# Prompt attention: normalising the softmax weights before their transposes instead of the outputs after the value products

## The chip, the cores and the metric

One core of one Trainium2 chip. The metric is device time in microseconds of one execution of the whole kernel, which computes one inference step of a one-layer hybrid encoder. All data are float32.

## The reference, cut to what matters

The layer has two parallel groups of heads, an output projection and a feed-forward block. The change touches only the prompt part of the attention group: 8 heads, 1,024 queries, 1,040 keys (16 learned tokens and 1,024 frames), block-causal by chunks of 64.

```python
def attend_block(qn, qr, q_chunk, kn, kr, v, k_chunk):
    s = jnp.einsum('bqhd,bkhd->bhqk', qn, kn) + jnp.einsum('bqhr,bkr->bhqk', qr, kr)
    s = s.astype(jnp.float32) * ATTN_SCALE
    mask = k_chunk[None, :] <= q_chunk[:, None]
    s = jnp.where(mask[None, None], s, NEG)
    p = jax.nn.softmax(s, axis=-1).astype(v.dtype)
    return jnp.einsum('bhqk,bkhd->bqhd', p, v)
```

The outputs of all heads then pass through an RMS norm and, beside the other group's outputs, the output projection.

## The kernel before, in words

The kernel has three stages, one after the other: `layer_inputs` (input projection, the recurrent heads, the sample's attention), `prompt_attention` and `tail` (output projection and feed-forward block). The change is in `prompt_attention`.

**Tiles and steps.** Heads are taken in four pairs. A step is one head of the pair (`a`, 0 or 1) and one tile of 128 queries (`t`, 0 to 7). Tile `t` sees `144 + 128 t` keys (`width[t]`), cut into 1 score unit for tiles 0 to 2, 2 units for tiles 3 to 6 and 3 units for tile 7. A pair has 16 steps in an order written out by hand, which puts a long tile beside a short one:

```python
ORDER = ((0, 7), (0, 0), (1, 7), (0, 1), (0, 6), (1, 0), (1, 6), (1, 1),
         (0, 5), (0, 2), (1, 5), (0, 3), (0, 4), (1, 2), (1, 4), (1, 3))
MIX = ((3, 7), (0, 10), (2, 15), (1, 18))
LAG, BANKS, TURN = 2, 5, 5
```

**What a step does.** TensorE multiplies queries and keys (L1937) into one of five PSUM banks, queries on partitions; the mask comes with eight extra rows of the operands. VectorE takes each row's maximum (L2100 for one unit; L2102 for each of several and L2105 over them). ScalarE writes the exponentials to `pq` and their sum for each unit to `sums` (L2024). TensorE transposes the weights by 128x128 blocks, in groups of up to four (L1949), into banks 5 and 6, and VectorE and ScalarE copy the groups to `pT` (L2012 and L2017): for tiles 4 to 7 ScalarE the first and third group and VectorE the second, for tiles 0 to 3 VectorE the first and ScalarE any other.

**The value products.** For two query tiles at once (`m` = 0 to 3) and both heads of the pair, `mix` multiplies V and the transposed weights into bank 7 (L1967); the output has the two heads' 64 values on partitions and 256 queries in columns. There are four in a pair, 16 in all, placed by `MIX` after the steps 7, 10, 15 and 18, counted from the first step of the pair.

**Normalisation.** Queries are columns there, while the sums lie with queries on partitions. So VectorE adds the parts of the sums for two tiles and two heads (L2113) and takes reciprocals (L2115). GpSimd widens each reciprocal to 64 columns (`wide`, L2076). TensorE transposes `wide` into the other half of bank 7, two transposes before each value product (L1958). ScalarE copies that half to `spread` (L2017, called by `widened`). VectorE multiplies output and `spread` into `g.mixT` (L2119).

**The order of work around it.** Each engine runs its instructions in order and waits on semaphores. In iteration i of the loops, TensorE does scores(i), the transposes of step i-2, then a value product if one is placed there. VectorE does the maxima of step i, its copies for step i-2, sums and reciprocals of a pair of tiles just finished, and the output multiplication of a value product one iteration older. ScalarE does its copies for step i-2, the exponentials of step i, then the copy of `spread`. Steps share four slots of maxima (`RINGS`). SyncE's queue loads the next heads' V after `m_ps` has counted the last value product of a pair.

Behind these loops, ScalarE squares each pair's outputs (L2036), GpSimd adds the squares up (L2061), TensorE sums them over partitions and already does the other group's part of the output projection (L1974); VectorE multiplies the outputs by the norm (L2141).

Of the kernel before, what the change touches and what calls it, by code (L numbers as in the profile page):

```python
# [11 lines left out]
P = 128  # L12
# [1802 lines left out]
def prompt_attention(nc, g, io, phase):  # L1815
# [19 lines left out]
    part = sb("part", [P, RINGS, 3])  # L1835
    neg = sb("neg", [P, RINGS])
    sums = sb("sums", [P, 2, QT_N, 2, 3])
    total = sb("total", [P, 2, QT_N, 2])
    rec = sb("rec", [P, 2, QT_N, 2])
    wide = [sb(f"wide{i}", [P, 2 * P]) for i in range(2)]  # L1840
    spread = [sb(f"spread{i}", [P, 2 * P]) for i in range(2)]
    sq = sb("sq", [P, SEQ])
    acc = sb("acc", [P, SEQ])
    norm = sb("norm", [P, QT_N])
# [33 lines left out]
    ready = {}  # L1878
    for pair in range(PAIRS):
        for j, (m, _) in enumerate(MIX):  # L1880
            last = max(x for x, (_, t) in enumerate(ORDER) if t // 2 == m)
            ready.setdefault(pair * len(ORDER) + last, []).append((pair, m, 4 * pair + j))
    done_at = {n: i for i, found in ready.items() for _, _, n in found}
    END = max(mixes) + 1
    s = {n: sem("a_" + n) for n in """qk_in0 qk_in1 qk_in2 qk_in3 v_in0 v_in1 v_in2 v_in3 rw_in m_in fixed s_ps part_ok neg_ok e_ok t_ps
        ta_ok tv_ok tot_ok rec_ok wide_ok m_ps sp_ok o_ok sq_ok acc_ok ss_ps ms_ok pow_ok bc_ps mix_ok zero new_ok wo_in""".split()}
    block = phase.block()

    def turned(n):
# [37 lines left out]
    def _(pe):  # L1927
# [12 lines left out]
        def turns(i):  # L1940

            _, a, t = steps[i]
            pe.wait_ge(s["e_ok"], unit_at[i + 1])
            for j, (k0, k1) in enumerate(groups[i]):
                n = group_at[i] + j
                if n >= 2:
                    pe.wait_ge(*turned(n - 2))
                for k in range(k0, k1):
                    last = pe.transpose(pb[TURN + n % 2][:, (k - k0) * P:(k - k0 + 1) * P], rows_of(a, t)[:, k * P:(k + 1) * P], ident)  # L1949
                last.then_inc(s["t_ps"], 1)  # L1950

        def mix(pair, m, n):
            out, done = pb[7], group_at[done_at[n] + 1]
            pe.wait_ge(s["wide_ok"], n + 1)
            if n:
                pe.wait_ge(s["o_ok"], n)
            for x in range(2):
                pe.transpose(out[:, 2 * P + x * P:3 * P + x * P], wide[n % 2][:, x * P:x * P + P], ident)  # L1958
            pe.wait_ge(s["ta_ok"], act_before[done])
            pe.wait_ge(s["tv_ok"], done - act_before[done])  # L1960
            for a in range(2):
                head = 2 * pair + a
                pe.wait_ge(s[f"v_in{head % 4}"], head // 4 * 32 + 32)
            for k in range(2 * m + 3):
                x = max(0, P * k - CHUNK - 2 * P * m)
                for a in range(2):
                    last = pe.matmul(out[64 * a:64 * a + 64, x:2 * P], vh[(2 * pair + a) % 4][0:size[k], k, :],  # L1967
                                     cols_of(a, m)[0:size[k], k, x:], start=k == 0, stop=True, skip_group_check=k > 0)
            last.then_inc(s["m_ps"], 1)
# [45 lines left out]
    @block.scalar  # L2015
    def _(act):
        copy = lambda out, in_: act.activation(out, in_, ACT.Copy)  # L2017

        def weights(i):
            pair, a, t = steps[i]  # L2020
            act.wait_ge(s["neg_ok"], i + 1)
            for u in range(units[i]):
                n, x, y = unit_at[i] + u, cuts[t][u], cuts[t][u + 1]
                act.activation(rows_of(a, t)[:, x:y], pb[n % BANKS][:, 0:y - x], ACT.Exp, bias=neg[:, i % RINGS:i % RINGS + 1],  # L2024
                               accum_out=sums[:, pair % 2, t, a, u:u + 1]).then_inc(s["e_ok"], 1)

        def widened(n):
            act.wait_ge(s["m_ps"], n + 1)
            copy(spread[n % 2][:, :], pb[7][:, 2 * P:4 * P]).then_inc(s["sp_ok"], 1)

        def squares(j):
            act.wait_ge(s["o_ok"], 4 * j + 4)
            if j:
                act.wait_ge(s["acc_ok"], j)
            out = sq if j else acc
            act.activation(out[:, :], g.mixT[:, j, 0:SEQ], ACT.Square).then_inc(s["sq_ok"], 1)  # L2036

        for b in range(4):
            rows = slice(QKD, ROWS)
            q0, k0 = CON["q_mask"][0], CON["k_mask_rows"][0]  # L2040
            act.dma_start(qT[b][rows, :], io.con[rows, q0:q0 + SEQ]).then_inc(s["m_in"], 16)
            act.dma_start(kT[b][rows, :], io.con[rows, k0:k0 + KEYS]).then_inc(s["m_in"], 16)
        act.wait_ge(s["zero"], 1)
        for i in range(END + LAG + 1):
            j = i - LAG
            if 0 <= j < N:
                turn_out(act, copy, j, True)
            if i < N:
                weights(i)
            for _, _, n in mixes.get(j - 1, ()):  # L2050
                widened(n)
                if n % 4 == 0 and n:
                    squares(n // 4 - 1)
        squares(PAIRS - 1)

    @block.gpsimd
    def _(pool):
# [10 lines left out]
                pool.memset(rows_of(a, t)[:, width[t]:], 0.0).then_inc(s["fixed"], 1)  # L2068
        pool.tensor_copy(g.mixT[:, 0:4, SEQ:], g.mix_s[:, :, :]).then_inc(s["new_ok"], 1)
        for pair in range(PAIRS):  # L2070
            for j, (m, _) in enumerate(MIX):
                n = 4 * pair + j
                pool.wait_ge(s["rec_ok"], n + 1)
                if n >= 2:
                    pool.wait_ge(s["m_ps"], n - 1)
                pool.tensor_copy(wide[n % 2][:, :].rearrange("p (t a d) -> p t a d", t=2, a=2),  # L2076
                                 bcast(rec[:, pair % 2, 2 * m:2 * m + 2, :], 3, VD)).then_inc(s["wide_ok"], 1)
            if pair:
                add_squares(pair - 1)
        add_squares(PAIRS - 1)  # L2080
# [5 lines left out]
    def _(dve):  # L2086
# [17 lines left out]
            dve.wait_ge(s["part_ok"], n_part)  # L2104
            dve.tensor_reduce(own, part[:, r, 0:units[i]], AX.X, ALU.max, negate=True).then_inc(s["neg_ok"], 1)  # L2105

        n_rec = 0

        def factors(pair, m):
            nonlocal n_rec  # L2110
            n_rec += 1
            c = slice(2 * m, 2 * m + 2)
            dve.tensor_reduce(total[:, pair % 2, c, :], sums[:, pair % 2, c, :, :], AX.X, ALU.add).then_inc(s["tot_ok"], 1)  # L2113
            dve.wait_ge(s["tot_ok"], n_rec)
            dve.reciprocal(rec[:, pair % 2, c, :], total[:, pair % 2, c, :]).then_inc(s["rec_ok"], 1)  # L2115

        def outputs(pair, m, n):
            dve.wait_ge(s["sp_ok"], n + 1)
            dve.tensor_tensor(g.mixT[:, pair, 2 * P * m:2 * P * m + 2 * P], pb[7][:, 0:2 * P], spread[n % 2][:, :], ALU.mult  # L2119
                              ).then_inc(s["o_ok"], 1)  # L2120

        dve.memset(sums[:, :, :, :, :], 0.0).then_inc(s["zero"], 1)
        for i in range(END + LAG + 1):
            j = i - LAG
            if i < N:
                maxima(i)
            if 0 <= j < N:
                turn_out(dve, dve.tensor_copy, j, False)
            for pair, m, _ in ready.get(j, ()):
                dve.wait_ge(s["e_ok"], unit_at[j + 1])  # L2130
                factors(pair, m)
            for found in mixes.get(j - 1, ()):
                outputs(*found)
        dve.wait_ge(s["ss_ps"], 1)
        dve.tensor_scalar(norm[:, :], pb[7][:, 0:QT_N], 1.0 / MLA_OUT, EPS, ALU.mult, ALU.add).then_inc(s["ms_ok"], 1)
        dve.wait_ge(s["rw_in"], 48)
# [646 lines left out]
```

## Time and profile before

| what | before |
|---|---|
| median of 3 runs | 1870.22 us (1868.64 to 1870.82) |
| profiled execution, its own time | 1871.17 us |
| its span, first to last instruction | 1869.2 us |
| mean granted TensorE clock | 0.973 |
| TensorE busy | 1760.5 us (94%) |
| VectorE busy | 962.3 us (51%) |
| ScalarE busy | 402.8 us (22%) |
| GpSimd busy | 603.0 us (32%) |

The profile is one execution. PE is TensorE (PEld its weight loads), DVE VectorE, ACT ScalarE, POOL GpSimd, SP SyncE. L1937 is line 1937 of the kernel before. A line of a view gives an engine, a line, an operation, output and input by name, shapes and a count. TensorE's records overlap, since products are pipelined and their ends are modelled: the time that an instruction holds the engine is read from one start to the next. A float32 score or value product is two records, a transpose one.

### The profile page before, as it was taken

The numbers are of one execution on the slowest core, as the hardware profiler recorded it, in microseconds if no ns is written. First come the engines' busy times: TensorE is split into PE (matmuls) and PEld (weight loads), VectorE is DVE, ScalarE is ACT, GpSimd is POOL, SyncE is SP. The second block draws the span as 40 slices with busy tenths as digits, with TensorE's granted clock in tenths as the row PEclk, the third lists the DMA queues.
The fourth block names the chain that finished last, engine by engine and source line by source line (L and its number), as shares of the span: only waits on it lengthen the run. The fifth ranks groups of instructions, "written<-read, shape, count | busy, mean of one in ns | idle before, by whom it ended". The sixth has DMA issues, their size and how long they took to land.

```text
span 1869.2 us, 34786 instructions
## 1 busy us (share of the span) xinstructions
PE 1760.5 (94%) x14813; PEld 1338.2 (72%) x14813; DVE 962.3 (51%) x1766; ACT 402.8 (22%) x942; POOL 603.0 (32%) x418
## 2 busy tenths in 40 slices
PE   5899999999997886999899899999999999999998
PEld 3566666666665654666566788888888888888887
DVE  2757767767767674656334534434443343725322
ACT  2333333333333223555101111000100010000000
POOL 2554663664545440000120111222222111734432
PEclk9999999999997797999999999999999999999999
DMA  9343243234222006210230211011111111333431
GB/s 379 116 154 105 67 150 105 86 131 137 84 89 66 21 7 162 56 47 1 92 114 16 100 45 46 24 44 46 46 45 46 46 44 35 121 121 116 140 93 59
DMA packets 71035, 158.92 MB, mean 85 GB/s; under 512 B 19353, under 2 KB 47849, under 8 KB 66658
## 3 DMA queue, kind: packets, MB, share of 16 engines
q1 hardware_dynamic: 66866, 115.74, 19.3%
q10 hardware_dynamic: 4016, 40.96, 6.2%
q8 instruction: 118, 1.93, 0.4%
q14 instruction: 35, 0.29, 0.0%
HBM read 128.57 MB, written 20.44 MB: 80 GB/s over the span
## 4 chain that ended last, share of the span: by engine, by line
PE 50%; DVE 1%; issue 0%; ACT 0%; DVEq 0%
PE psum L2313 44%; PE psum L2292 5%; PE psum L2302 0%; DVE u_sum L2539 0%; DVE u_sum L2544 0%; DVE mixT L2540 0%; PE psum L2308 0%; DVE mixT L2523 0%; DVE rb L2556 0%; DVE hid L2520 0%; DVE hid L2519 0%; DVE hid L2515 0%; DVE yout L2656 0%; DVE part L2655 0%; DVE part L2605 0%
## 5 line engine op out<-in xcount | busy, mean ns | idle before, releaser
L2313 PE MATMUL psum<-mixT,wA 128*128 128x264 f32 x1408 | 337.3, 388 | 1.9 <-DVE rb L2556 1.5
L2313 PEld LDWEIGHTS psum<-mixT,wA 128*128 128x128 f32 x1408 | 268.4, 191 | 48.6 <-DVE rb L2556 1.7
L2313 PE MATMUL psum<-u_sum,wA 128*128 128x264 f32 x1232 | 297.2, 386 | 0.5 <-DVE u_sum L2539 0.5
L445 PE MATMUL psum<-wsl,xt 128*128 128x368 f32 (+1 forms) x1092 | 284.1, 455 | 8.4 <-DMA wsl<-in_w_in 5.2
L2313 PEld LDWEIGHTS psum<-u_sum,wA 128*128 128x128 f32 x1232 | 234.3, 190 | 41.0 <-issue 0.9
L445 PEld LDWEIGHTS psum<-wsl,xt 128*128 128x128 f32 (+1 forms) x1092 | 149.9, 173 | 90.8 <-issue 17.6
L2470 POOL TENSOR_TENSOR wA<-wA 128x512 f32<-128x512 f32 x22 | 28.5, 1296 | 427.1 <-DMA wA<-in_w_gate 231.2
L2313 PE MATMUL psum<-hid,wA 128*128 128x264 f32 x528 | 120.3, 386 | 2.1 <-DVE hid L2607 1.5
L2313 PEld LDWEIGHTS psum<-hid,wA 128*128 128x128 f32 x528 | 100.2, 190 | 19.9 <-issue 2.8
L1937 PE MATMUL psum<-kT,qT 104*128 104x346 f32 (+7 forms) x224 | 78.4, 469 | 13.8 <-DMA kT<-in_con 13.8
L1286 POOL TENSOR_TENSOR Ls<-Lraw,con 128x512 f32<-128x512 f32 x45 | 49.2, 1102 | 106.2 <-ACT Lraw L953 76.3
L2313 PE MATMUL psum<-mixT,u_sum 128*128 128x264 f32 x352 | 79.8, 386 | 0.0
L2313 PEld LDWEIGHTS psum<-mixT,u_sum 128*128 128x128 f32 x352 | 66.8, 190 | 11.7 <-POOL u_sum L2490 0.3
L2437 ACT ACTIVATE p<-psum 128x264 f32<-128x264 f32 x44 | 17.2, 390 | 253.6 <-PE psum L2313 253.4
L1252 POOL TENSOR_TENSOR st<-st,con 128x3 f32<-128x3 f32 (+1 forms) x18 | 50.7, 2817 | 59.8 <-DVE st L1449 30.6
L2024 ACT ACTIVATE pq<-psum,neg 128x346 f32<-128x346 f32 (+7 forms) x112 | 59.7, 541 | 33.5 <-DVE neg L2105 25.2
L2102 DVE TENSOR_REDUCE part<-psum 128x1 f32<-128x347 f32 (+5 forms) x88 | 43.7, 523 | 44.7 <-PE psum L1937 43.9
L953 ACT ACTIVATE proj<-psum,rstd 128x368 f32<-128x368 f32 (+1 forms) x72 | 36.9, 512 | 138.1 <-PE psum L445 137.5
L1949 PEld LDWEIGHTS psum<-con,pq 128*128 128x128 f32 x352 | 41.2, 141 | 29.9 <-issue 10.1
L1949 PE MATMUL psum<-con,pq 128*128 128x128 f32 x352 | 52.8, 276 | 9.3 <-DVE pT L2012 5.4
L2480 POOL TENSOR_TENSOR wA<-wA 128x1408 f32<-128x1408 f32 x8 | 25.5, 3189 | 108.1 <-DMA wA<-in_w_down 108.1
L2570 DVE TENSOR_TENSOR part<-psum,p 128x264 f32<-128x264 f32 x44 | 19.0, 432 | 79.1 <-PE psum L2313 79.1
(354 smaller groups left out, 2870.0 us busy)
## 6 DMA issues: line engine op xcount, KB each, us to landing
wsl<-in_w_in ACTq DMA_DIRECT2D x27, 1472.0 KB, 6.6
wA<-in_w_down SPq DMA_DIRECT2D x32, 704.0 KB, 4.2
wA<-in_w_gate SPq DMA_DIRECT2D x22, 512.0 KB, 4.4
wA<-in_w_up SPq DMA_DIRECT2D x22, 512.0 KB, 4.3
mixed<-proj SPq DMA_DIRECT2D x8, 784.0 KB
xt<-in_x_tiles SPq DMA_DIRECT2D x9, 512.0 KB, 6.0
wsl<-in_w_in SPq DMA_DIRECT2D x3, 1472.0 KB, 13.6
out_y<-hid SPq DMA_DIRECT2D x1, 4224.0 KB, 12.0
```

The source lines that it names most:

```text
L445: return pe.matmul(out, lhsT, rhs, start=start, stop=stop)
L953: copy = lambda out, in_, **k: act.activation(out, in_, ACT.Copy, **k)
L1252: tt(out, ms, c_("minus_half")[:, 0:n], ALU.pow).then_inc(s[ok], 1)
L1286: tt(Ls[i % 2][:, :, :], Lraw[:, :, :], bcast(c_("levels")[:, i * 64:(i + 1) * 64], 1, H), ALU.mult).then_inc(s["Ls_ok"], 1)
L1937: pe.matmul(pb[n % BANKS][:, 0:y - x], qT[b][0:ROWS, t * P:(t + 1) * P], kT[b][0:ROWS, x:y], start=True, stop=True).then_inc(s["s_ps"], 1)
L1949: last = pe.transpose(pb[TURN + n % 2][:, (k - k0) * P:(k - k0 + 1) * P], rows_of(a, t)[:, k * P:(k + 1) * P], ident)
L2024: act.activation(rows_of(a, t)[:, x:y], pb[n % BANKS][:, 0:y - x], ACT.Exp, bias=neg[:, i % RINGS:i % RINGS + 1], accum_out=sums[:, pair % ...
L2102: dve.tensor_reduce(part[:, r, u:u + 1], src, AX.X, ALU.max).then_inc(s["part_ok"], 1)
L2292: last = pe.matmul(pb[3 * b + n][:, 0:TN], wo[u % 4][:, k, :], g.mixT[:, k, n * TN:(n + 1) * TN], start=k == 0 and u >= 2, stop=k == end - ...
L2313: ins = pe.matmul(pb[bank][:, 0:NW], left(k), right(k), start=first and k == 0, stop=k == depth - 1, skip_group_check=not first)
L2470: tt(S1, A21, A22, ALU.add).then_inc(s["s1_ok"], 1)
L2480: tt(Ahi[:, 0:FH], Alo[:, 0:FH], Ahi[:, 0:FH], ALU.subtract).then_inc(s["e3_ok"], 1)
```

## The change

The weights of a step are divided by their row's sum as soon as its exponentials are there, with queries still on partitions, and before they are transposed. VectorE does it in `scaled(i)`: it adds the parts of the sum if the tile has more than one unit, takes a reciprocal of 128x1, and multiplies the step's whole rows in place. TensorE's transposes of a step wait for that (`n_ok`) where they waited for its exponentials. VectorE's iteration is now maxima of step i, `scaled(i-1)`, copies of step i-2. Sums and reciprocals by pairs of tiles, `wide`, its transposes, `spread` and the output multiplication are gone; the output needs only a copy from bank 7 to `g.mixT`, which ScalarE does where it copied `spread`. Outputs alternate between two halves of bank 7.

```diff
-    total = sb("total", [P, 2, QT_N, 2])
-    rec = sb("rec", [P, 2, QT_N, 2])
-    wide = [sb(f"wide{i}", [P, 2 * P]) for i in range(2)]
-    spread = [sb(f"spread{i}", [P, 2 * P]) for i in range(2)]
+    total = sb("total", [P, RINGS])
+    rec = sb("rec", [P, RINGS])
...
         def turns(i):
...
-            pe.wait_ge(s["e_ok"], unit_at[i + 1])
+            pe.wait_ge(s["n_ok"], i + 1)
...
         def mix(pair, m, n):
-            out, done = pb[7], group_at[done_at[n] + 1]
-            pe.wait_ge(s["wide_ok"], n + 1)
+            out, done = pb[7][:, n % 2 * 2 * P:n % 2 * 2 * P + 2 * P], group_at[done_at[n] + 1]
             if n:
                 pe.wait_ge(s["o_ok"], n)
-            for x in range(2):
-                pe.transpose(out[:, 2 * P + x * P:3 * P + x * P], wide[n % 2][:, x * P:x * P + P], ident)
...
-        def widened(n):
+        def outputs(pair, m, n):
             act.wait_ge(s["m_ps"], n + 1)
-            copy(spread[n % 2][:, :], pb[7][:, 2 * P:4 * P]).then_inc(s["sp_ok"], 1)
+            copy(g.mixT[:, pair, 2 * P * m:2 * P * m + 2 * P], pb[7][:, n % 2 * 2 * P:n % 2 * 2 * P + 2 * P]).then_inc(s["o_ok"], 1)
...
-            for j, (m, _) in enumerate(MIX):
-                n = 4 * pair + j
-                pool.wait_ge(s["rec_ok"], n + 1)
-                if n >= 2:
-                    pool.wait_ge(s["m_ps"], n - 1)
-                pool.tensor_copy(wide[n % 2][:, :].rearrange("p (t a d) -> p t a d", t=2, a=2),
-                                 bcast(rec[:, pair % 2, 2 * m:2 * m + 2, :], 3, VD)).then_inc(s["wide_ok"], 1)
...
-        def factors(pair, m):
...
-            dve.tensor_reduce(total[:, pair % 2, c, :], sums[:, pair % 2, c, :, :], AX.X, ALU.add).then_inc(s["tot_ok"], 1)
-            dve.wait_ge(s["tot_ok"], n_rec)
-            dve.reciprocal(rec[:, pair % 2, c, :], total[:, pair % 2, c, :]).then_inc(s["rec_ok"], 1)
-
-        def outputs(pair, m, n):
-            dve.wait_ge(s["sp_ok"], n + 1)
-            dve.tensor_tensor(g.mixT[:, pair, 2 * P * m:2 * P * m + 2 * P], pb[7][:, 0:2 * P], spread[n % 2][:, :], ALU.mult
-                              ).then_inc(s["o_ok"], 1)
+        def scaled(i):
+
+            nonlocal n_tot
+            pair, a, t = steps[i]
+            r, found = i % RINGS, sums[:, pair % 2, t, a, :]
+            dve.wait_ge(s["e_ok"], unit_at[i + 1])
+            if units[i] > 1:
+                dve.tensor_reduce(total[:, r:r + 1], found[:, 0:units[i]], AX.X, ALU.add).then_inc(s["tot_ok"], 1)
+                n_tot += 1
+                dve.wait_ge(s["tot_ok"], n_tot)
+                found = total[:, r:r + 1]
+            dve.reciprocal(rec[:, r:r + 1], found[:, 0:1]).then_inc(s["rec_ok"], 1)
+            dve.wait_ge(s["rec_ok"], i + 1)
+            w = rows_of(a, t)[:, 0:width[t]]
+            dve.tensor_scalar(w, w, rec[:, r:r + 1], None, ALU.mult).then_inc(s["n_ok"], 1)
...
             if i < N:
                 maxima(i)
+            if 0 <= i - 1 < N:
+                scaled(i - 1)
             if 0 <= j < N:
                 turn_out(dve, dve.tensor_copy, j, False)
-            for pair, m, _ in ready.get(j, ()):
-                dve.wait_ge(s["e_ok"], unit_at[j + 1])
-                factors(pair, m)
-            for found in mixes.get(j - 1, ()):
-                outputs(*found)
```

## Rows read from the trace of the kernel before

**Rows 1.** Timeline 775 to 797 us: start, length, engine, line, operation, idle before

```profile
780.31 0.42 DVE L2119 TENSOR_TENSOR mixT<-psum,spread 128x256 f32<-128x256 f32 x1 [2.07 <-ACT spread L2017]
...
787.95 0.68 DVE L2012 COPY pT<-psum 128x512 f32<-128x512 f32 x1
...
788.55 0.43 DVE L2100 TENSOR_REDUCE neg<-psum 128x1 f32<-128x272 f32 x1
...
791.44 0.15 DVE L2113 TENSOR_REDUCE total<-sums 128x4 f32<-128x12 f32 x1
...
791.63 0.18 DVE L2115 RECIPROCAL rec<-total 128x4 f32<-128x4 f32 x1
```

**Rows 2.** Timeline 814 to 838 us, the same columns

```profile
815.89 2.02 PE L1937 MATMUL psum<-kT,qT 104*128 104x346 f32 x6
...
817.75 1.04 PE L1949 MATMUL psum<-con,pq 128*128 128x128 f32 x8
...
819.57 0.55 ACT L2024 ACTIVATE pq<-psum,neg 128x346 f32<-128x346 f32 x1
...
821.05 0.22 ACT L2024 ACTIVATION_READ_ACCUMULATOR pq<-psum,neg 128x1 f32 x1
...
821.58 0.42 DVE L2119 TENSOR_TENSOR mixT<-psum,spread 128x256 f32<-128x256 f32 x1 [2.07 <-ACT spread L2017]
...
823.66 0.38 PE L1958 MATMUL psum<-con,wide 128*128 128x128 f32 x2
...
823.98 1.96 PE L1967 MATMUL psum<-pT,vh 128*64 128x256 f32 x20
...
828.07 1.04 PE L1949 MATMUL psum<-con,pq 128*128 128x128 f32 x8
...
828.95 0.62 PE L1937 MATMUL psum<-kT,qT 104*128 104x272 f32 x2
...
833.96 3.83 PE L1967 MATMUL psum<-pT,vh 128*64 128x256 f32 x36
...
837.72 0.60 PE L1937 MATMUL psum<-kT,qT 104*128 104x392 f32 x1
```

**Rows 3.** Windows: busy PE, PEld, DVE, ACT, POOL; granted clock, DMA, GB/s

```profile
785.00:826.30 41.30, 38.32 (x250) 26.46 (x249) 25.14 (x66) 23.28 (x73) 1.61 (x4) 1.00 0.21 52
```

**Rows 4.** Waits from 735 to 900 us: total, times, longest

```profile
DVE mixT L2119 <- ACT spread L2017: 16.3, 15, 2.7
...
PE psum L1949 <- DVE pT L2012: 5.4, 7, 0.8
...
PE psum L1958 <- POOL wide L2076: 2.9, 7, 0.6
```

**Rows 5.** Groups by line and shape, 725 to 925 us: busy, mean ns, idle before

```profile
L2102 DVE TENSOR_REDUCE part<-psum 128x1 f32<-128x347 f32 x16 | 8.0, 515 | 1.8 <-PE psum L1937 1.5
...
L2061 POOL TENSOR_TENSOR acc<-acc,sq 128x1024 f32<-128x1024 f32 x3 | 7.1, 2357 | 6.2 <-ACT sq L2036 6.2
L2119 DVE TENSOR_TENSOR mixT<-psum,spread 128x256 f32<-128x256 f32 x16 | 6.8, 425 | 20.5 <-ACT spread L2017 20.5
...
L2115 DVE RECIPROCAL rec<-total 128x4 f32<-128x4 f32 x16 | 2.8, 178 | 0.6
L2113 DVE TENSOR_REDUCE total<-sums 128x4 f32<-128x12 f32 x16 | 2.5, 155 | 0.0
```

**Rows 6.** Groups by line and shape, VectorE, whole span

```profile
L2523 DVE TENSOR_SCALAR mixT<-hid,g_ffn 128x1056 f32<-128x1056 f32 x2 | 1.4, 766 | 4.1 <-PE psum L2292 4.1
...
L1518 DVE TENSOR_SCALAR sig<-sig,con 128x512 f32<-128x512 f32 x1 | 0.5, 485 | 0.0
L1700 DVE TENSOR_SCALAR wsl<-con,wsl 128x128 f32<-128x128 f32 x2 | 0.5, 286 | 0.0
```

**Rows 7.** Timeline 74 to 77.5 us

```profile
74.99 1.59 DVE L1580 TENSOR_SCALAR kK<-kK,con 128x512 f32<-128x512 f32 x1
75.04 1.27 POOL L1340 TENSOR_TENSOR rR<-rR,mixed 128x512 f32<-128x512 f32 x1 [1.74 <-DVE aA L1572]
```

More of the change, by code:

```diff
@@ L1880, in prompt_attention @@
         for j, (m, _) in enumerate(MIX):
-            last = max(x for x, (_, t) in enumerate(ORDER) if t // 2 == m)
+            last = max(x for x, (_, u) in enumerate(ORDER) if u // 2 == m)
             ready.setdefault(pair * len(ORDER) + last, []).append((pair, m, 4 * pair + j))
@@ L1885, in prompt_attention @@
     s = {n: sem("a_" + n) for n in """qk_in0 qk_in1 qk_in2 qk_in3 v_in0 v_in1 v_in2 v_in3 rw_in m_in fixed s_ps part_ok neg_ok e_ok t_ps
-        ta_ok tv_ok tot_ok rec_ok wide_ok m_ps sp_ok o_ok sq_ok acc_ok ss_ps ms_ok pow_ok bc_ps mix_ok zero new_ok wo_in""".split()}
+        ta_ok tv_ok tot_ok rec_ok n_ok m_ps o_ok sq_ok acc_ok ss_ps ms_ok pow_ok bc_ps mix_ok zero new_ok wo_in""".split()}
     block = phase.block()
@@ L2049, in _ @@
                 weights(i)
-            for _, _, n in mixes.get(j - 1, ()):
-                widened(n)
+            for pair, m, n in mixes.get(j - 1, ()):
+                outputs(pair, m, n)
                 if n % 4 == 0 and n:
@@ L2105, in maxima @@
             dve.tensor_reduce(own, part[:, r, 0:units[i]], AX.X, ALU.max, negate=True).then_inc(s["neg_ok"], 1)
-        n_rec = 0
-        def factors(pair, m):
-            nonlocal n_rec
-            n_rec += 1
-            c = slice(2 * m, 2 * m + 2)
-            dve.tensor_reduce(total[:, pair % 2, c, :], sums[:, pair % 2, c, :, :], AX.X, ALU.add).then_inc(s["tot_ok"], 1)
-            dve.wait_ge(s["tot_ok"], n_rec)
-            dve.reciprocal(rec[:, pair % 2, c, :], total[:, pair % 2, c, :]).then_inc(s["rec_ok"], 1)
-        def outputs(pair, m, n):
-            dve.wait_ge(s["sp_ok"], n + 1)
-            dve.tensor_tensor(g.mixT[:, pair, 2 * P * m:2 * P * m + 2 * P], pb[7][:, 0:2 * P], spread[n % 2][:, :], ALU.mult
-                              ).then_inc(s["o_ok"], 1)
+        n_tot = 0
+        def scaled(i):
[12 more added lines that the diff above has]
+            dve.tensor_scalar(w, w, rec[:, r:r + 1], None, ALU.mult).then_inc(s["n_ok"], 1)
         dve.memset(sums[:, :, :, :, :], 0.0).then_inc(s["zero"], 1)
```

## The prediction, made before the changed kernel was run

> **What bounds the kernel now.** I read the page first. TensorE is busy 94% of the span, so elsewhere a microsecond counts only where it makes TensorE wait. Then I read the windows. Prompt attention works through four equal head pairs. A pair lasts 41.27 us, from one multiplication of an output to the same one a pair later (780.31 and 821.58) [rows 1, 2]. In it TensorE is busy 38.32 us, VectorE 25.14, ScalarE 23.28, and the granted clock is 1.00, the 2.4 GHz level [rows 3].
>
> The timeline shows TensorE's share of a pair by starts, since durations overlap. Three score units of 1,039 columns hold it 1.86 us (815.89 to 817.75), so the 9,472 score columns of a pair take 16.9. Eight transposes hold it 0.88 us, so 88 take 9.7. The 36 records of the longest value product hold it 3.76 us, so the 96 of a pair take 10.0. Two transposes of widened reciprocals hold it 0.32 us, four times 1.3 [rows 2]. Together that is 37.9, and 3.4 us of a pair are pauses. The waits name them [rows 4]: over the stage 5.4 us for VectorE's copies, 2.9 for the widened reciprocals, and smaller ones. VectorE itself sat 16.3 us waiting for ScalarE's copy of the spread reciprocals, with its copies queued behind; that wait was 2.07 us just before 821.58 [rows 2], and TensorE's wait for a copy follows it. So this stage is bound by TensorE, with pauses from the path being given up.
>
> **What is removed.** On TensorE, 32 transposes: 4 x 1.3 = 5.2 us; the wait for GpSimd, 2.9; most of the wait for copies behind the output multiplication, up to 5.4. That is 13.5 us; a pipeline that stops also refills, so I allow up to 19. On VectorE 16 output multiplications (6.8 us), 16 reciprocals (2.8) and 16 sums (2.5): 12.1 us, 3.0 a pair [rows 5]. ScalarE's 16 copies of 256 columns become 16 copies of 256 columns into the output: nothing, with ScalarE idle 18 of 41 us to cover it [rows 3]. GpSimd's 16 widenings cost nothing by themselves. No DMA is added or moved; the loads of V still wait for the same product. The two halves of bank 7 gain little, as the product still waits for the output before it.
>
> **What is added, all on VectorE's queue.** In each of 64 steps, one reciprocal and one in-place scaling of the step's whole weight rows (144 to 1,040 columns), and in the 40 steps with more than one score unit a sum. Scaling with a factor per partition is shown at 128 columns (286 ns), 512 (485) and 1,056 (766) [rows 6]: 286 ns plus 0.517 ns a further column. The 64 scalings cover 37,888 columns: 18.3 + 15.4 = 33.7 us. How instructions follow each other is in the timeline: the next independent one starts 0.08 us before the record ends (787.95 + 0.68, next at 788.55), a dependent one 0.04 us after (791.44 + 0.15, next at 791.63) [rows 1]. So scalings hold the queue 33.7 - 5.1 = 28.6 us, 64 reciprocals 0.19 each 12.2 (a 128x1 one is not shown in this stage; 178 ns is the row of 128x4, hardly less), 40 sums 7.6. That is 48.4 us, 12.1 a pair. VectorE goes from 25.1 to 25.1 - 3.0 + 12.1 = 34.2 us of a pair, TensorE's own work falls to 36.6. Neither total exceeds 41.3, so order decides.
>
> **Order.** In iteration i TensorE does scores(i), transposes(i-2), and four times a pair a value product; VectorE does maxima(i), then scales step i-1, then copies its part of i-2. The scaling waits for ScalarE's exponential of i-1; behind it on VectorE stand the copy and the next maxima. TensorE's transposes(i-2) now wait for the scaling of i-2, and behind them stand the value product and the next scores. VectorE's reductions and copies from PSUM cost 0.15 us and 1.05 ns a column (272: 0.43, 512: 0.68, 347: 0.515) [rows 1, 5]. For query tiles 0 to 7 that makes, less the overlaps, maxima 0.26, 0.35, 0.48, 0.87, 1.00, 1.16, 1.27, 1.50 (tile 7: 3 x 0.515 + 0.155 less 0.2); scaling with reciprocal and sum 0.40, 0.47, 0.54, 0.79, 0.86, 0.92, 0.99, 1.07; copies 0.34, 0.47, 0.60, 0.60, 0.34, 0.47, 0.60, 0.60. The order pairs a long tile with a short one: 7 with 0, 7 with 1, 6 and 0, 6 and 1, 5 and 2, 5 and 3, 4 and 2, 4 and 3. These eight blocks hold VectorE 4.2, 4.5, 3.9, 4.2, 4.2, 4.8, 3.8, 4.5 = 34.1 us, which agrees with 34.2. In the tile 7 blocks a loop is longer: scaling 1.07, short copy 0.34, maxima 1.50, exponentials 1.70 (819.57 to 821.27) and ScalarE's own copies ahead of them [rows 2], about 4.8 and 4.9; for tile 6, by its columns, 4.1 and 4.2. With these the blocks are 35.3. TensorE's own blocks are 3.0 to 3.7, so outside value products VectorE sets the pace.
>
> During a value product no score comes, and VectorE has at most one iteration left. The four hold TensorE 3.8, 2.9, 2.1 and 1.2 us (by their 36, 28, 20 and 12 records). The longest, and 1.0 until the next score unit lands, stands against 1.9 us of work: 2.9 idle. The second with 0.9 against 2.1: 1.7. The third, with transposes that end 1.3 late ahead of it and 0.6 for the next unit, against 2.7: 1.3. The shortest: none. With these 5.9 a pair takes 35.3 + 5.9 = 41.2 us against 41.27. **What the path given up saves on TensorE is given back by VectorE.** Over four pairs: -0.3 us.
>
> At the start the first scaling stands before the first transpose and delays the third maxima: +1.7 (its own 1.07, the rest as the queues fill). At the end two transposes less, one scaling more: -0.2 together.
>
> **A shared resource.** Two GpSimd additions of 1,024 columns, 2.36 us each [rows 5], fall inside the loop. The trace shows a scaling of 512 columns with a factor per partition taking 1.59 us where GpSimd began an operation of 1.27 us at the same moment [rows 7], against 0.485 without [rows 6]. So a scaling that meets an addition loses between 0 and 2.36 us; I take 0.75 each, since part of it is idle time anyway: +1.5. Of this the Trainium skill speaks against the change (SBUF — State Buffer, "Who interferes with whom"): a scaling by VectorE that uses both its ports and a GpSimd operation exclude each other for a whole instruction, and whichever came first wins. By that both additions could hold VectorE to the full, and the sum would be 3.2 us longer; the one slow scaling in the trace agrees, having lost 1.11 us.
>
> **Sum:** -0.3 + 1.7 - 0.2 + 1.5 = +2.7 us on the profiled execution (1871.17, its span 1869.2). The median shown is 1870.22, so 1873.
>
> **Rivals.** *TensorE stays the bound.* For it: VectorE has 34.2 us of work in 41, and if maxima and scaling fill the value products the pauses vanish. Then 13.5 to 19 us go: 1870.2 - 16 = 1854. Against it: a value product holds up scores too. *The exponential joins every loop (slower).* Scaling(i-1) at the head of VectorE's queue waits for ScalarE, which first copies its transposes of i-2, which now wait for a scaling. In my sum this path is 0.3 us shorter than VectorE's own in the blocks of tiles 4 to 6. Once transposes start more than 0.3 us after their scaling, as when TensorE is still in a score or value product, each block pays; at 0.6 us a block, 32 blocks: +19, so 1889. ScalarE's free 18 us speak against it. *Scaling does not run at the rate of rows 6*, because it is in place or reads its factor just written: at twice the time a column, +15 us on VectorE, mostly on its path: 1885. The 512 and 1,056 rows speak against it.
>
> **How the numbers follow.** A difference of 0.2%, 3.7 us, is about what a measurement of this kernel can tell from no change. My forecast, the balance at 1873 with its own range of 1865 to 1880, gets 0.44, split 0.06 faster, 0.26 same, 0.12 slower. TensorE bound gets 0.24, exponential in the loop 0.22, slow scaling 0.10. Faster 0.30, same 0.26, slower 0.44. The range 1856 to 1890 takes in the slower cases and the weaker half of the fast one.
>
> **What would show it.** Right: VectorE busy 34 us a pair, widened transposes gone, TensorE busy about 37 of 41 with new waits of transposes on the scaling line, 8 to 12 us in all or more, and the wait for the spread copy gone. A scaling of 528 columns near 0.49 us, one of 1,040 near 0.76. Wrong toward fast: pairs of 38 us, TensorE hardly waiting for the scaling. Wrong toward slow: VectorE waiting for ScalarE's exponential in most steps and pairs of 43 to 46 us, or scalings over 1 us. Outside this stage nothing should move.

## The result, and the profile after

The changed kernel takes 1880.32 us (median of 5 runs, 1875.17 to 1880.68) against 1870.23 us, a ratio of 1.0051 with a 95% interval of 1.004 to 1.0062: slower by half a per cent, some 9.5 us. The forecast was 1873 within 1856 to 1890, with slower the likeliest of the three.

| what | before | after |
|---|---|---|
| profiled execution, own time | 1871.17 us | 1880.32 us |
| its span | 1869.2 us | 1878.3 us |
| VectorE busy | 962.3 us | 1000.5 us |
| first score product to last value product | 168.87 us | 179.58 us |
| a head pair in the middle | 41.26 us | 43.12 us |

The last two lines come from timelines. The stage is measured from the start of the first score product (730.19 now, 731.45 before) to the start of the last value product (900.32 before). A pair is measured between the same maxima of tile 7, as at 780.26 and 823.38 below. Every pair length in what follows is such a difference. Of the 10.7 us by which the stage grew, the profiled execution shows 9.15 in the whole time; most of the rest is that this stage began 1.26 us earlier, after a part of the kernel that the change does not touch. TensorE's last value product, first in the kernel before, then in the changed one, and behind them the two maxima of tile 7 that bound a pair of the kernel before:

```profile
900.32 1.96 PE L1967 MATMUL psum<-pT,vh 128*64 128x256 f32 x20
...
909.77 1.96 PE L1962 MATMUL psum<-pT,vh 128*64 128x256 f32 x20
...
775.58 1.62 DVE L2102 TENSOR_REDUCE part<-psum 128x1 f32<-128x346 f32 x3 [3.39 <-PE psum L1937]
...
816.84 1.62 DVE L2102 TENSOR_REDUCE part<-psum 128x1 f32<-128x346 f32 x3 [3.42 <-PE psum L1937]
```

Next VectorE's timeline of the changed kernel over one pair, cut to the instructions before which it stood idle (start, length, operation, idle before and who ended it), with one more maximum of tile 7, at 816.59, for comparison:

```profile
780.26 1.62 DVE L2090 TENSOR_REDUCE part<-psum 128x1 f32<-128x346 f32 x3 [1.72 <-PE psum L1935]
...
783.36 0.44 DVE L2088 TENSOR_REDUCE neg<-psum 128x1 f32<-128x272 f32 x1 [0.29 <-PE psum L1935]
...
784.72 0.16 DVE L2104 TENSOR_REDUCE total<-sums 128x1 f32<-128x3 f32 x1 [0.92 <-ACT pq L2019]
...
790.03 0.31 DVE L2088 TENSOR_REDUCE neg<-psum 128x1 f32<-128x144 f32 x1 [1.49 <-PE psum L1935]
...
803.11 1.15 DVE L2090 TENSOR_REDUCE part<-psum 128x1 f32<-128x392 f32 x2 [3.14 <-PE psum L1935]
...
810.44 0.57 DVE L2088 TENSOR_REDUCE neg<-psum 128x1 f32<-128x400 f32 x1 [0.35 <-PE psum L1935]
...
816.59 1.36 DVE L2090 TENSOR_REDUCE part<-psum 128x1 f32<-128x346 f32 x3
...
819.91 0.16 DVE L2104 TENSOR_REDUCE total<-sums 128x1 f32<-128x3 f32 x1 [0.43 <-ACT pq L2019]
...
823.38 1.62 DVE L2090 TENSOR_REDUCE part<-psum 128x1 f32<-128x346 f32 x3 [1.72 <-PE psum L1935]
```

VectorE is idle 8.34 us of the 43.12: 1.72, 1.49 and 3.14 us until scores arrive after three of the value products, 1.35 us for tile 7's exponentials, 0.64 in two short gaps. The other 34.8 us are its own queue; the two add up to the pair by the way they are read. A little waiting hides in the 34.8: three maxima of tile 7 take 1.62 us at 780.26, where each waits for its scores, and 1.36 at 816.59, where all scores are there. With the like at 803.11 (1.15 us, and 1.03 for the same two maxima at 795.82) that is 0.4 us, so the work itself is about 34.4.

A window as long as that pair, begun 3 us earlier (busy TensorE, its weight loads, VectorE, ScalarE, GpSimd; granted clock; DMA share; GB/s) answers to [rows 3]:

```profile
777.20:820.30 43.10, 38.12 (x244) 25.71 (x240) 33.36 (x96) 23.34 (x75) 0.00 (x0) 1.00 0.19 46
```

VectorE went from 25.14 to 33.36 us. TensorE executes eight transposes fewer, and yet its records cover 38.12 us, hardly less than 38.32. A transpose's record lasts 0.27 us, though eight of them hold TensorE for 0.88, so the last record before each pause counts as busy while nothing new starts. A busy TensorE here is not a working one.

The groups by line and shape (total, mean ns, idle before) answer to [rows 5, 6]:

```profile
L2108 DVE RECIPROCAL rec<-total 128x1 f32<-128x1 f32 x40 | 6.6, 164 | 1.4
...
L2111 DVE TENSOR_SCALAR pq<-pq,rec 128x1040 f32<-128x1040 f32 x8 | 6.1, 761 | 0.3
...
L2104 DVE TENSOR_REDUCE total<-sums 128x1 f32<-128x2 f32 x32 | 4.7, 146 | 0.8 <-ACT pq L2019 0.4
...
L2111 DVE TENSOR_SCALAR pq<-pq,rec 128x528 f32<-128x528 f32 x8 | 4.4, 551 | 0.3
...
L2111 DVE TENSOR_SCALAR pq<-pq,rec 128x144 f32<-128x144 f32 x8 | 2.4, 295 | 0.3
```

The scaling costs what the rows of before said: 761 ns for 1,040 columns against 757 worked out (286 + 0.517 x 912), 295 ns for 144 against 294. Only that of 528 columns lies over its 493, and two instances of 0.68 and 0.75 us are why (below). The waits from 735 to 905 us (total, times, longest) answer to [rows 4]:

```profile
PEld psum L1947 <- DVE pq L2111: 36.0, 37, 1.7
...
PE psum L1947 <- DVE pq L2111: 14.8, 25, 1.5
DVE total L2104 <- ACT pq L2019: 6.9, 9, 1.6
...
PE psum L1947 <- DVE pT L2007: 3.8, 6, 0.8
```

The waits for widened reciprocals and for the spread copy are gone. In their place TensorE waits 14.8 us in 25 places for scaled weights. Its next weight load waits 36.0 us for the same, much of it beside products still in the pipeline.

### The profile page after: what moved, and what is told of

Read it like the earlier page. It is cut to its first block, busy times and chain, and to the rows that moved or that the text cites. A ratio compares the mean times of both kernels' runs of the same rounds, so it can differ in the third digit from the quotient of the medians.

```text
span 1878.3 us, 34798 instructions
## 1 busy us (share of the span) xinstructions
PE 1763.1 (94%) x14781; PEld 1337.3 (71%) x14781; DVE 1000.5 (53%) x1886; ACT 403.3 (21%) x942; POOL 596.6 (32%) x402
## 4 chain that ended last, share of the span: by engine, by line
PE 49%; DVE 1%; issue 0%; ACT 0%; DVEq 0%
PE psum L2301 44%; PE psum L2280 5%; PE psum L2290 0%; DVE u_sum L2527 0%; DVE u_sum L2532 0%; DVE mixT L2528 0%; PE psum L2296 0%; DVE mixT L2511 0%; DVE rb L2544 0%; DVE hid L2508 0%; DVE hid L2507 0%; DVE hid L2503 0%; DVE part L2643 0%; DVE yout L2644 0%; DVE part L2593 0%
## 5 line engine op out<-in xcount | busy, mean ns | idle before, releaser
L445 PE MATMUL psum<-wsl,xt 128*128 128x368 f32 (+1 forms) x1092 | 287.9, 459 | 8.9 <-DMA wsl<-in_w_in 5.6
L2301 PEld LDWEIGHTS psum<-mixT,u_sum 128*128 128x128 f32 x352 | 66.8, 190 | 11.7 <-POOL u_sum L2478 0.3
L1947 PEld LDWEIGHTS psum<-con,pq 128*128 128x128 f32 x352 | 39.9, 141 | 47.9 <-DVE pq L2111 36.0
L1947 PE MATMUL psum<-con,pq 128*128 128x128 f32 x352 | 53.5, 280 | 20.6 <-DVE pq L2111 14.8
L2056 POOL TENSOR_TENSOR acc<-acc,sq 128x1024 f32<-128x1024 f32 x3 | 7.1, 2356 | 188.1 <-ACT sq L2031 188.1
L2468 POOL TENSOR_TENSOR wA<-wA 128x1408 f32<-128x1408 f32 x8 | 25.7, 3208 | 112.1 <-DMA wA<-in_w_down 112.1
```

Source lines behind the costliest of these rows:

```text
L445: return pe.matmul(out, lhsT, rhs, start=start, stop=stop)
L2301: ins = pe.matmul(pb[bank][:, 0:NW], left(k), right(k), start=first and k == 0, stop=k == depth - 1, skip_group_check=not first)
L2468: tt(Ahi[:, 0:FH], Alo[:, 0:FH], Ahi[:, 0:FH], ALU.subtract).then_inc(s["e3_ok"], 1)
```

## The experiments

**Theory 1:** VectorE's queue sets the pace of a pair: its work, plus the time in which no scores come because TensorE is in a value product. **Theory 2:** it is the chain of waits (exponential, sum, reciprocal, scaling, transposes) that sets it, whatever the scaling costs the queue. Ratios are to the kernel before, with 95% intervals. Single runs of one kernel spread over up to 10 us here, so the pair lengths from the traces carry the verdicts beside them.

**Removal alone.** Nothing is divided in this kernel.

```diff
-            pe.wait_ge(s["n_ok"], i + 1)
+            pe.wait_ge(s["e_ok"], unit_at[i + 1])
...
-            if 0 <= i - 1 < N:
-                scaled(i - 1)
```

> The changed kernel without sums, reciprocals and scaling on VectorE: transposes wait for the exponentials as before the change, and the weights are left undivided. It prices the removal alone. Both theories: the widened path was worth 13.5 to 19 us, so 1852 to 1857, with pairs of about 37.5 us and hardly a wait of TensorE.

1856.92 us, ratio 0.9928 (0.99 to 0.9956). Two maxima of tile 7 a pair apart:

```profile
770.12 1.62 DVE L2090 TENSOR_REDUCE part<-psum 128x1 f32<-128x346 f32 x3 [3.02 <-PE psum L1935]
...
807.46 1.61 DVE L2090 TENSOR_REDUCE part<-psum 128x1 f32<-128x346 f32 x3 [3.02 <-PE psum L1935]
```

A pair is 37.34 us and the stage 153.86 (728.85 to 882.71), so the path given up was worth 15.0 us of stage, inside the 13.5 to 19 of the forecast; by the ratio of the times it is 13.5, with an interval of 8 to 19. The change had this much and more to pay: what it adds costs 179.58 - 153.86 = 25.7 us.

**The scaling's length.** The weights beyond the first two columns of a row stay undivided.

```diff
-            w = rows_of(a, t)[:, 0:width[t]]
+            w = rows_of(a, t)[:, 0:2]
```

> The changed kernel with each scaling cut to 2 columns (the other weights are left undivided); every instruction, its place in the queue and every semaphore stay. Theory 1, VectorE's occupancy sets the pair: the 64 scalings fall from 0.53 to about 0.2 us each, 5 us of VectorE a pair, and the pair falls from 43.1 to about 38.5, so 1858 to 1863. Theory 2, the chain of waits itself (exponential, sum, reciprocal, scaling, then transposes) sets it whatever the scaling's length: pairs stay above 41.5, so 1872 or more.

1864.18 us, ratio 0.9974 (0.9963 to 0.9986), 1 us over the expected range; pairs of 39.9 us:

```profile
771.38 1.62 DVE L2090 TENSOR_REDUCE part<-psum 128x1 f32<-128x346 f32 x3 [2.00 <-PE psum L1935]
...
811.28 1.03 DVE L2090 TENSOR_REDUCE part<-psum 128x1 f32<-128x346 f32 x2 [1.99 <-PE psum L1935]
```

All instructions and waits of the chain are there, and 3.2 of the 5.8 us between 37.34 and 43.12 are gone. That is against theory 2 in its strong form. A shorter scaling also shortens the chain, though, so this run alone does not part the theories; the next one does. The remaining 2.6 us a pair are what three short instructions a step cost, occupancy and waits together.

**Work without the wait.**

```diff
-            pe.wait_ge(s["n_ok"], i + 1)
+            pe.wait_ge(s["e_ok"], unit_at[i + 1])
...
-            w = rows_of(a, t)[:, 0:width[t]]
+            w = scratch[:, 0:width[t]]
```

> The changed kernel with each scaling done on a scratch tile of the same size; transposes wait for the exponentials alone, and the weights are left undivided. VectorE has all its work in the same order, but nobody waits for the scaling itself. Theory 1 (occupancy of VectorE's queue, with the copies and maxima behind the scaling): pairs of 41.5 to 43, so 1872 to 1879. Theory 2 (the wait for the scaled weights): pairs of about 38.5, so 1857 to 1863.

1876.14 us, ratio 1.0029 (1.0014 to 1.0044):

```profile
778.05 1.62 DVE L2091 TENSOR_REDUCE part<-psum 128x1 f32<-128x346 f32 x3 [1.62 <-PE psum L1936]
...
820.50 1.62 DVE L2091 TENSOR_REDUCE part<-psum 128x1 f32<-128x346 f32 x3 [1.62 <-PE psum L1936]
```

With nobody waiting for the scaling a pair is still 42.45 us. The wait of the transposes is worth 0.67 us a pair; the other 5.1 us are the work on the queue together with VectorE's own waits for tile 7's exponentials, which this kernel keeps (1.35 us). VectorE's queue takes 34.8 us of the pair here too. This run settles it for theory 1. The waits of TensorE for scaled weights, the largest new entry in the waits, mark where the delay shows and not what makes it.

**Order within VectorE's queue.**

```diff
-            if 0 <= i - 1 < N:
-                scaled(i - 1)
             if 0 <= j < N:
                 turn_out(dve, dve.tensor_copy, j, False)
+            if 0 <= i - 1 < N:
+                scaled(i - 1)
```

> The changed kernel with VectorE's copies of step i-2 ahead of the scaling of step i-1 in its queue. Theory 1: the total is the same but the copy now waits for transposes that were released late, so about the same or slower, pairs of 42.5 to 45. Theory 2: VectorE's waits for the exponential of the longest tiles (1.4 us a pair) shrink and pairs fall by up to 1.4 us, time by up to 5 us.

1897.56 us, ratio 1.0154 (1.0131 to 1.0178), worse than expected. The pair from 773.72 to 818.40 is 44.68 us, the top of the range. The next, from 818.40 to 866.48, is 48.08, and holds this:

```profile
853.06 2.34 POOL L2056 TENSOR_TENSOR acc<-acc,sq 128x1024 f32<-128x1024 f32 x1 [131.66 <-ACT sq L2031]
853.22 2.61 DVE L2111 TENSOR_SCALAR pq<-pq,rec 128x784 f32<-128x784 f32 x1
855.75 0.89 DVE L2090 TENSOR_REDUCE part<-psum 128x1 f32<-128x328 f32 x2
```

GpSimd's addition began 0.16 us ahead of a scaling that otherwise takes 0.63 us; the scaling took 2.61 and ended 0.43 us after the addition. The pair is 3.4 us longer: 2.0 are the scaling's, and 1.5 more are waits of VectorE for TensorE (10.58 us of idle time in the pair, 9.07 in the one before). They go with a lower clock: TensorE waited 2.62 us for this scaling, and when it went on it was granted 1.2 GHz for some 3 us, in which a value product of 12 records took 1.74 us in place of 1.09. One of its windows:

```profile
856.00:857.00 1.00, 1.00 (x5) 1.00 (x6) 0.80 (x3) 0.00 (x0) 0.00 (x0) 0.50 0.00 0
```

Whether such a collision comes about is decided by when the two start.

**A value product behind the next scores.** In TensorE's queue each value product moves behind the scores of the next iteration, and what is done with its output moves one iteration later.

```diff
+            for found in mixes.get(j - 1, ()):
+                mix(*found)
             if 0 <= j < N:
                 turns(j)
...
-            for found in mixes.get(j, ()):
-                mix(*found)
```

> The changed kernel with each value product moved behind the next step's scores in TensorE's queue, and the output copy one iteration later; all results are computed. Theory 1 with its second term (VectorE, which sets the pace, sits idle about 6.3 us of each pair because no scores come during a value product): with one more step's maxima and scaling to do meanwhile, pairs fall from 43.1 to 38.5 to 40.5 us, so 1860 to 1869, which would be faster than both kernels. Rival: the idle time in the products only moves elsewhere, since transposes still wait for scalings made in order: pairs of 42.5 or more, 1876 or more.

1878.79 us, ratio 1.0048 (1.0032 to 1.0064): missed. Its pairs are 41.60 and, with an addition of GpSimd in the way of a scaling, 43.28 us (766.49, 808.09, 851.37). That scaling took 2.18 us in place of 0.49, the clock stayed at 2.4 GHz, and the pair grew by just this 1.7. VectorE's timeline says where the idle time went:

```profile
796.73 0.56 DVE L2007 COPY pT<-psum 128x384 f32<-128x384 f32 x1 [2.50 <-PE psum L1947]
...
816.81 0.69 DVE L2007 COPY pT<-psum 128x512 f32<-128x512 f32 x1 [1.80 <-PE psum L1947]
```

The waits for scores have shrunk from 7.0 to 0.7 us, but the copies now wait for transposes, which stand behind the value product instead. 1.5 us of a pair are won in the trace (3.5 us of stage); the timed runs don't show it, and the profiled execution was the fastest of its seven, 7 us under their median. The rival was the nearer one here: by the time it holds, while the pairs of 41.60 lie between the two expectations.

**The same move before the change.**

> The same move in the kernel before the change, whose VectorE is busy only 25 of 41 us a pair and does not set the pace. Theory 1: little to win from VectorE, the pair loses only part of its waits for copies behind the output multiplication: 1863 to 1871. Rival (any kernel of this stage gains from keeping VectorE fed in the products): as much as the changed kernel, 8 us or more.

1866.09 us, ratio 0.9983 (0.9973 to 0.9992), with pairs of 39.55 us (767.30 to 806.85) against 41.26. So this order is worth 1.7 us of a pair there, as much as in the changed kernel. The time lies in theory 1's range, but my reason for expecting little, that VectorE doesn't set that kernel's pace, is not borne out. Since both kernels gain as much, the gain says nothing about which of them VectorE paces. Which wait pays for it was not followed up.

**A longer distance between scores and transposes.**

```diff
-    LAG, BANKS, TURN = 2, 5, 5
+    LAG, BANKS, TURN = 3, 5, 5
```

> The changed kernel with transposes and copies three steps behind the scores in place of two. Theory 1: TensorE's waits for the scaled weights move, but VectorE's work is the same; it gains only where it waited for exponentials (1.4 us a pair) and by one more step in hand at a product: pairs of 40.5 to 43, 1868 to 1880. Theory 2 (the latency from scores to scaled weights): pairs of 38.5, 1860.

1891.39 us, ratio 1.012 (1.0103 to 1.0137), outside every expectation: pairs of 43.21 and 46.49 us (770.03, 813.24, 859.73), the second one again with an addition, under which the mean of the 528-column scalings rises to 1026 ns; as in the kernel with the copies first, a stretch at 1.2 GHz follows the collision (granted clock 0.50 from 854 to 856). One more step of room for the chain wins nothing. Why even the undisturbed pair did not gain was not followed up.

**The scaling on GpSimd.**

```diff
-            w = rows_of(a, t)[:, 0:width[t]]
-            dve.tensor_scalar(w, w, rec[:, r:r + 1], None, ALU.mult).then_inc(s["n_ok"], 1)
...
+        for i in range(N):
+            _, a, t = steps[i]
+            pool.wait_ge(s["rec_ok"], i + 1)
+            w = rows_of(a, t)[:, 0:width[t]]
+            pool.tensor_scalar(w, w, rec[:, i:i + 1], None, ALU.mult).then_inc(s["n_ok"], 1)
+            if i % 16 == 12 and i > 16:
+                add_squares(i // 16 - 1)
```

> The changed kernel with the scaling itself on GpSimd; sums and reciprocals stay on VectorE. All results are computed. Theory 1: VectorE loses 7 us a pair and keeps 27.6, but GpSimd needs perhaps 1 to 2 us for a long tile, from its 1.3 us for 512 columns of two tensors, and transposes wait for it: if it keeps up, pairs of 38 to 40 us and 1857 to 1867; if its total passes 40 us a pair it becomes the bound and the time goes over 1890.

1935.05 us, ratio 1.0348 (1.0333 to 1.0364). The groups of its GpSimd:

```profile
L2069 POOL TENSOR_SCALAR pq<-pq,rec 128x1040 f32<-128x1040 f32 x8 | 23.4, 2922 | 30.7 <-DVE rec L2112 30.7
...
L2069 POOL TENSOR_SCALAR pq<-pq,rec 128x144 f32<-128x144 f32 x8 | 5.1, 643 | 10.5 <-DVE rec L2112 10.5
```

A long tile takes 2.92 us there, over my 1 to 2. GpSimd is not full: its scalings add up to 28 us of a pair of 52.9 (784.62 to 837.53). But transposes, copies and the next maxima stand behind each: in this pair TensorE waits 11.7 us for scaled weights and VectorE 11.7 for transposes to copy. So here theory 2's chain does bind, at four times the length of a scaling. A part is the clock: its granted mean over this pair was 0.94, against 1.00 in the undisturbed pairs of the others, and that part was not priced.

**Less work for VectorE.** The copies of tiles 0 to 3 go to ScalarE.

```diff
-        if len(groups[i]) == 3:
-            by_act[i][2] = True
+        if len(groups[i]) == 3 or t < 4:
+            by_act[i] = [j != 1 or t < 4 for j in range(len(groups[i]))]
```

> The changed kernel with VectorE's copies for tiles 0 to 3 (their first groups) given to ScalarE, which is busy 23 of 43 us a pair; all results are computed. Theory 1 (VectorE's queue sets the pace): it loses 4.0 us a pair and ScalarE takes 4; pairs fall from 43.1 to 39 to 40.5 us, so 1862 to 1869. Rival (waits between engines, not VectorE's load): pairs of 42 or more, 1874 or more, as ScalarE's exponentials come later.

1871.34 us, ratio 1.0012 (1.0 to 1.0023): 7 us or so better than the changed kernel, 2 us over the expected range. Pairs are 41.07 us. The maxima that bound one, and three of VectorE's waits around it:

```profile
766.02 1.36 DVE L2090 TENSOR_REDUCE part<-psum 128x1 f32<-128x346 f32 x3
...
782.60 0.31 DVE L2088 TENSOR_REDUCE neg<-psum 128x1 f32<-128x144 f32 x1 [1.83 <-PE psum L1935]
...
794.99 1.15 DVE L2090 TENSOR_REDUCE part<-psum 128x1 f32<-128x392 f32 x2 [3.60 <-PE psum L1935]
...
807.09 1.36 DVE L2090 TENSOR_REDUCE part<-psum 128x1 f32<-128x346 f32 x3
...
813.89 1.62 DVE L2090 TENSOR_REDUCE part<-psum 128x1 f32<-128x346 f32 x3 [2.32 <-PE psum L1935]
```

Of 4.0 us taken off the queue a pair won 2.05. The waits at value products grew from 1.49, 3.14 and 1.72 to 1.83, 3.60 and 2.32 us: work moved off a queue that has to wait for another one anyway is won in part only.

**Both.** The changed kernel with the copies moved and with the value products behind the next scores.

> That kernel with the value products behind the next step's scores as well. Theory 1: VectorE's queue is 30.8 us a pair and its idle time in the products falls, so TensorE's 36.6 us come near: pairs of 38 to 39.5 us, 1857 to 1864. Rival: the waits move only, pairs as without the move.

1869.18 us, ratio 0.9996 (0.9985 to 1.0007), pairs of 40.13 us (769.56 to 809.69): the changed arithmetic can be brought level with the kernel before, and not further in this way. My range was 5 us too low.

**The control.** The same copies moved in the kernel before the change.

> A control: the same copies moved from VectorE to ScalarE in the kernel before the change. Theory 1: VectorE does not set its pace, so within 3 us of it either way, 1866 to 1873. Rival (VectorE's copies hold up any version): pairs fall by 2 us or more, under 1863.

1869.09 us, ratio 1.0 (0.9989 to 1.0011), pairs of 40.85 us:

```profile
764.51 1.58 DVE L2102 TENSOR_REDUCE part<-psum 128x1 f32<-128x346 f32 x3
...
805.36 1.58 DVE L2102 TENSOR_REDUCE part<-psum 128x1 f32<-128x346 f32 x3
```

The move that gains 2.05 us a pair in the changed kernel gains 0.4 here. VectorE sets the pace of the one and not of the other. Theory 1 rests on this control and on the run with the scratch tile.

**A version that beats both.** The kernel before, with the value products behind the next scores and, on ScalarE, this:

```diff
+            for _, _, n in mixes.get(j - 2, ()):
+                widened(n)
             if i < N:
                 weights(i)
             for _, _, n in mixes.get(j - 2, ()):
-                widened(n)
```

> The kernel before the change with the value products behind the next step's scores, and ScalarE's copy of the spread reciprocals ahead of the exponentials of its iteration. It takes VectorE's wait for that copy, 4.4 us a pair in the version without this step, off its queue: pairs of 38.3 to 39.5 us against 39.5, 1860 to 1866. If exponentials delayed by the copy cost as much, 1866 to 1869.

1860.43 us, ratio 0.9947 (0.9932 to 0.9962), with pairs of 38.14 us (764.58 to 802.72). The wait behind which VectorE's copies had been queued, 4.4 us of one pair without this step, in its pair from 762 to 800 us:

```profile
DVE mixT L2120 <- ACT spread L2017: 1.1, 2, 0.9
```

This is 0.8 us a pair above the kernel that doesn't divide at all. What the change wanted to be rid of was mostly a matter of order.

## Why the prediction was right or wrong

**What is removed: right.** 13.5 to 19 us were allowed, and 15.0 measured in the stage.

**VectorE's added work: right, slightly low.** I had 34.2 us of a pair in its queue (34.1 by blocks, which is what the pair sum used) and the trace has 34.8, 0.4 of them hidden waits. Scalings cost what neighbouring rows said, within 4 ns where undisturbed. Sums and reciprocals are 9 and 14 ns shorter than the larger ones of [rows 5] and hold the queue the 0.17 to 0.20 us that I had. By its own formula my 0.26 for the maximum of tile 0 should be 0.22, too little to matter.

**The waits at value products: the term that was a little short.** I had 2.9, 1.7, 1.3 and 0 us; the timeline has 3.14, 1.72, 1.49 and none, 0.45 more. Waits for exponentials cost 1.35 us, all at tile 7, against the 1.2 that I had for tiles 7 and 6; for tile 6 the prediction charged 0.2 in its sum and called the same path shorter than VectorE's in its rival, and the trace has no wait there. The smaller waits, 0.64, I had not counted. With the 0.65 of the queue, 0.4 of it the hidden waits, that makes 43.1 against my 41.2. The step of the prediction that failed is its pair sum, "35.3 + 5.9 = 41.2": the mechanism held in each of its parts, and each was 0.1 to 0.7 us low, all on the same side. Small waits add up only one way, and I charged none. Against the 41.26 of before, a pair grew by 1.86 us where I had -0.07; four pairs make 7.4 of the 10.7 us by which the stage grew.

**The total: inside the range, in part by luck.** I had +2.7 us for the profiled execution, and it has +9.15. The balance that I favoured had its own range of 1865 to 1880, and 1880.32 lies at its very end. The wide range of 1856 to 1890 reached that far for two rivals that did not come true. Of my signs of being wrong toward slow, pairs of 43 to 46 us came with 43.12, but VectorE's wait for exponentials in most steps did not. TensorE's waits for the scaling are 14.8 us where I had 8 to 12 or more.

**The start: mis-sized.** I had +1.7 us. From the first maximum of tile 7 to the same one a pair later was 35.82 us before (733.01 to 768.83) and 41.72 after (731.75 to 773.47): +5.90, of which 1.86 is a pair's ordinary share. So 4.0 us belong to the start. Part of it is the clock, in this execution. The windows of a microsecond of the changed kernel:

```profile
740.00:745.00 5.00, 3.62 (x17) 2.08 (x17) 4.01 (x12) 3.12 (x11) 0.00 (x0) 1.00 1.04 405
745.00:746.00 1.00, 0.61 (x4) 0.64 (x5) 0.57 (x3) 1.00 (x5) 0.00 (x0) 0.75 1.04 406
746.00:747.00 1.00, 1.00 (x3) 0.58 (x3) 0.93 (x4) 0.22 (x2) 0.00 (x0) 0.50 1.04 417
747.00:748.00 1.00, 1.00 (x2) 0.41 (x2) 0.62 (x2) 0.00 (x0) 0.00 (x0) 0.50 0.36 143
748.00:749.00 1.00, 1.00 (x3) 0.26 (x2) 0.45 (x1) 0.00 (x0) 0.00 (x0) 0.54 0.06 25
749.00:750.00 1.00, 1.00 (x10) 1.00 (x9) 0.80 (x3) 0.39 (x1) 0.00 (x0) 1.00 0.00 0
```

After 5 us in which it was busy 3.62, waiting for its first scaled weights, TensorE was granted the lower level, 1.2 GHz, for about 3 us; four score records took 3.15 us where 1.70 is usual, 1.45 more. The kernel before was busy 4.71 us of 740 to 745 and kept 2.4 GHz. But the kernel that scales a scratch tile was busy hardly more than the changed one in the same 5 us, 3.67, and it kept 2.4 GHz up to 750. So it is not shown what made the clock fall. The windows of that kernel:

```profile
740.00:745.00 5.00, 3.67 (x20) 2.43 (x21) 4.25 (x13) 3.23 (x13) 0.00 (x0) 1.00 1.04 399
745.00:750.00 5.00, 5.00 (x27) 3.23 (x25) 4.58 (x14) 2.99 (x11) 0.00 (x0) 1.00 0.53 211
```

Other executions of the changed kernel took 1875.2 and 1876.5 us against 1880.3 to 1880.7; only this one's trace is shown, and whether the clock makes that difference stays open.

**The end: right in sign.** I had -0.2; the last pair and the end grew 1.06 us together (859.70 to 909.77 against 851.31 to 900.32), 0.8 less than a pair's share.

**The shared resource: price too high, and luck.** I took +1.5. In the profiled execution two scalings of 528 columns took 0.68 and 0.75 in place of 0.49 us, 0.45 in all:

```profile
850.28 2.36 POOL L2056 TENSOR_TENSOR acc<-acc,sq 128x1024 f32<-128x1024 f32 x1 [129.68 <-ACT sq L2031]
...
852.25 0.68 DVE L2111 TENSOR_SCALAR pq<-pq,rec 128x528 f32<-128x528 f32 x1
...
893.47 2.36 POOL L2056 TENSOR_TENSOR acc<-acc,sq 128x1024 f32<-128x1024 f32 x1 [40.83 <-ACT sq L2031]
...
895.37 0.75 DVE L2111 TENSOR_SCALAR pq<-pq,rec 128x528 f32<-128x528 f32 x1
```

Each scaling began as the addition was ending (852.64 and 895.83). That only its end met them is luck of the order: in three reordered kernels the same addition hit squarely, at up to 2.2 us of a scaling and 1.7 to 3.4 us of a pair. Every loss of a scaling lies within my 0 to 2.36 us; the pair lost more only where the clock fell behind the collision, which I had not thought of. The Trainium skill's rule (SBUF — State Buffer, "Who interferes with whom"), that whichever of the two comes first holds the other for the whole instruction, agrees with the rows at 853.06 and 853.22. It can't be read off the starts when they lie close. The kernel with the longer distance has the scaling's record start first, by 0.02 us, and the scaling is still the one that was held:

```profile
895.09 2.65 DVE L2111 TENSOR_SCALAR pq<-pq,rec 128x528 f32<-128x528 f32 x1
...
895.11 2.34 POOL L2056 TENSOR_TENSOR acc<-acc,sq 128x1024 f32<-128x1024 f32 x1 [44.23 <-ACT sq L2031]
```

The same holds of the two rows that the prediction rests on [rows 7]: VectorE's record starts 0.05 us ahead there, so it shows a loss of 1.11 us and not that the first wins.

**The rivals.** TensorE as the bound fell: by the prediction's own sum it works 36.6 us, of a pair of 43.1. The exponential in every loop fell too: in the pair shown VectorE waits for it in the tile 7 steps alone. Slow scaling fell by its own rows. The chain is not free either: 0.67 us a pair are the transposes' wait for the scaling.

## What to carry to other kernels

Before arithmetic is moved to an engine whose total would still fit, add its queue up for the repeating piece of the schedule, and add the stretches in which its input can't come: here 34.8 us of work and 8.3 of waiting made 43.1, although no engine was full. Where a wait is to be got rid of, look first at what stands ahead of the waited-for instruction in its queue; two reorderings won 8 to 10 us without a change of the arithmetic, and replacing the path lost as much. The longest new wait in a profile names the place of a delay; only a run that keeps the work and drops the wait tells which of the two it is.

## What was not expected of the hardware

- A GpSimd addition of 1,024 columns that began 0.16 us earlier held a VectorE scaling of 784 columns to 2.61 us, from 0.63. One whose record began 0.02 us later held a scaling of 528 columns to 2.65, from 0.49.
- GpSimd scales 1,040 float32 columns in 2.92 us and 144 in 0.64, VectorE in 0.76 and 0.30.
- The granted clock fell to 1.2 GHz for some 3 us inside the stage, after 5 us in which TensorE's records covered 72%; four score records in it took nearly twice as long. With 73% in the same 5 us another kernel kept 2.4 GHz. In two kernels it fell behind a collision, after TensorE had waited 2.62 and 3.16 us for the held scaling or for the copy behind it, and the pair grew by 1.5 and 1.2 us more than the scaling was held.
